# Delta-rule heads of a diffusion block on one Trainium2 core: directions dense on the partitions, paired 64x64 products, the next head's preparation inside the scan

## The reference, cut to what matters

```
qkv = silu(centred_conv(qkv, conv_w[l]))
q = l2norm(q) * DK ** -0.5;  k = l2norm(k)
o_f, s_f = gated_delta_chunked(q, k, v, beta[0], g[0], s0[:, 0])
o_b, s_b = gated_delta_chunked(rev(q), rev(k), rev(v), rev(beta[1]), rev(g[1]), s0[:, 1])
o = rmsnorm(o_f + rev(o_b), dn_norm[l]) * silu(z)
```

```
tmat = eye + bc[..., :, None] * einsum(kc, kc) * dec_strict
sol = triangular_solve(tmat, concat([(bc * gam) * kc, bc * vc]))
wk, uv = sol[..., :DK], sol[..., DK:]
u_c = uv_c - wk_c @ s
o_c = gam_c * (q_c @ s) + aqk_c @ u_c
s = gend_c * s + kd_c.T @ u_c
```

## Time and profile before

| | |
|---|---|
| runs | 4628.4, 4628.9, 4632.2 us; median 4628.9 |
| profiled execution | span 4630.4 us from the first to the last instruction, between the lowest and the highest run; what lies around the span cannot be told apart from that spread |
| instructions | 60884 |
| busy | PE 3719.1 us (80%), PEld 2456.7 (53%), DVE 2039.8 (44%), ACT 1080.3 (23%), POOL 890.1 (19%) |
| head phase | from 282.6 us to about 2196 us of the span, 1913 us |

### The profile page before, as it was taken

The page is one execution under the profiler, slowest core; times in us unless marked ns, Lnnn a source line. Parts: engine busy times, 40 slices in busy tenths (PEclk is TensorE's granted clock), DMA queues, the critical chain, the costliest instruction groups (busy, mean ns, idle before and its releaser), DMA issues. The chain is left out here.

```text
span 4630.4 us, 60884 instructions
## 1 busy us (share of the span) xinstructions
PE 3719.1 (80%) x22132; PEld 2456.7 (53%) x22398; DVE 2039.8 (44%) x3322; ACT 1080.3 (23%) x1702; POOL 890.1 (19%) x1040
## 2 busy tenths in 40 slices
PE   6568788888888797976854544599999699999997
PEld 2237575756666666755444444355454355555554
DVE  1236565656556565655459999422311211111112
ACT  0323232333232323232210011133211321111112
POOL 0010000000000000000067788011111011111110
PEclk8789898898989898989876777799999899999998
DMA  6210000000000000000311111221112011111111
GB/s 244 71 33 1 11 17 11 17 11 17 11 17 10 19 10 19 10 18 8 96 40 25 24 27 26 94 86 59 41 36 85 20 41 37 41 41 39 38 35 56
DMA packets 224662, 178.59 MB, mean 39 GB/s; under 512 B 24005, under 2 KB 211478, under 8 KB 222166
## 3 DMA queue, kind: packets, MB, share of 16 engines
q1 hardware_dynamic: 218214, 153.89, 11.4%
q10 hardware_dynamic: 4608, 11.54, 0.6%
q0 software_dynamic: 1648, 10.54, 0.6%
HBM read 144.39 MB, written 27.33 MB: 37 GB/s over the span
## 5 line engine op out<-in xcount | busy, mean ns | idle before, releaser
L171 POOL TENSOR_TENSOR w_pair<-w_raw,w_pair 128x1024 bf16<-128x1024 f32 (+1 forms) x156 | 345.9, 2220 | 2542.1 <-ACT w_pair L166 2542.1
L182 PE MATMUL m_out<-hn,w_pair 128*128 128x512 bf16 (+1 forms) x3102 | 569.3, 343 | 36.3 <-PEq L152 32.9
L182 PE MATMUL bank<-hn,w_pair 128*128 128x512 bf16 (+1 forms) x2220 | 480.3, 361 | 93.7 <-ACTq L1086 71.5
L182 PEld LDWEIGHTS m_out<-hn,w_pair 128*128 128x128 bf16 x3168 | 310.3, 98 | 294.9 <-issue 34.5
L182 PEld LDWEIGHTS bank<-hn,w_pair 128*128 128x128 bf16 x2304 | 225.8, 102 | 296.9 <-issue 131.3
L182 PE MATMUL m_out<-ys,w_pair 128*128 128x512 bf16 (+1 forms) x1552 | 288.6, 346 | 16.9 <-DVE ys L1996 15.0
L166 ACT ACTIVATE w_pair<-w_raw 128x1024 bf16<-128x1024 f32 x156 | 163.0, 1050 | 413.5 <-PE m_out L182 254.2
L1992 DVE TENSOR_TENSOR m_a<-m_out,m_sg 128x1280 f32<-128x1280 f32 x22 | 32.8, 1492 | 483.7 <-PE m_out L182 483.7
L1688 PE MATMUL s_banks<-u_block,m_block 128*128 128x160 f32 x128 | 40.9, 412 | 250.2 <-DVEq L1794 250.2
L182 PEld LDWEIGHTS m_out<-ys,w_pair 128*128 128x128 bf16 x1584 | 156.0, 99 | 149.6 <-issue 21.3
L182 PE MATMUL b_out<-ys,w_pair 128*128 128x512 bf16 (+1 forms) x1132 | 210.5, 345 | 5.2 <-PEq L1242 4.0
(11 more groups left out here) (346 smaller groups left out, 6460.6 us busy)
## 6 DMA issues: line engine op xcount, KB each, us to landing
w_raw<-in_w_in SPq DMA_DIRECT2D x56, 512.0 KB, 3.9
w_ada_rows<-in_w_ada SPq DMA_DIRECT2D x16, 1536.0 KB, 6.6
w_raw<-in_w_gu SPq DMA_DIRECT2D x44, 512.0 KB, 3.9
w_raw<-in_w_down SPq DMA_DIRECT2D x16, 512.0 KB, 4.0
scratch_x<-x_t POOLq DMA_DIRECT2D x1, 5120.0 KB, 16.4
scratch_o<-o_pair ACTq DMA_DIRECT2D x8, 640.0 KB, 3.9
scratch_u<-u_rows ACTq DMA_DIRECT2D x8, 640.0 KB, 2.9
u_block<-scratch_u SPq DMA_DIRECT2D x128, 40.0 KB, 1.8
```

The source lines that it names most:

```text
L171: pool.tensor_tensor(K.w_pair[:, slot, 1, 0:kt, :], K.w_raw[:, slot, 0:kt, :], K.w_pair[:, slot, 0, 0:kt, :], ALU.subtract).then_inc(K.w_l ...
L182: mm = pe.matmul(out[:, c0:c0 + cn], K.w_pair[:, slot, w, k, :], x[:, a, k, c0:c0 + cn], start=i < 3, stop=i >= 9 * kt - 3)
```

## The change

`phase_heads` is rewritten, and what it takes from `phase_decays` with it (beta times the decay to the chunk's end is made there, the order of packs follows the scan's order).

- Dense directions. The forward matrix of a pack lies on partitions 0 to 63, the backward one on 64 to 127, each 64 columns wide: x, xt, w and the masked matrices are 128 x 20 x 64, half as many columns. A product is issued as a pair, one matmul per direction, on the array's 64x64 tile of its half; the pair of the inverse, of uv and of at by u writes two partition halves of one bank, the pairs of wk and of kd by u write two banks.
- Groups. The inverse goes in four groups of five packs (320 columns). The mask of a level is applied by POOL to mt ahead of the level (`masked`); DVE adds the identity to the first product (`evict_v`) and copies xt; ACT copies x (`copy_x`). POOL scales k (`scale`).
- z. The z tile is put in ten parts between the products of levels 1 to 5 (`z_part`).
- Scan. One instruction for u over all partitions, one output add for two steps. The next head's decay differences, its k, q and v tiles (8 matmuls at each of 27 places from step 0 on), its squares, sums and norms are in it.
- Tail. Square, sums, gate and split of a head are done within levels 1 to 4 of the next one.
- No `head_end`; the loop over heads is written out in full. Every bank has its own semaphore; one ring of five banks. State is kept twice; POOL issues its loads, ACT its stores in the scan.

The core of the diff (PE, ACT and DVE of the scan, PE of the inverse):

```diff
-                        for g in range(NG):
-                            pe.wait_ge(s.inv, NG * (LEVELS * h + l - 1) + g + 1)
-                            for t in range(4):
-                                mm = pe.matmul(b[:, t, :], mt[:, 4 * g + t, :], xi[:, 4 * g + t, :], start=True, stop=True)
...
+                    for l in range(1, LEVELS):
+                        for g, t0, n in FIVES:
+                            pe.wait_ge(s.m, NF * (LEVELS * h + l) + g + 1)
+                            pe.wait_ge(s.x, NF * ((LEVELS - 1) * h + l - 1) + g + 1)
+                            b = to_write(pe, "v", h, l, g)
+                            for t in range(n):
+                                for d in range(2):
+                                    mm = pe.matmul(cols(b, C)[half(d), t, :], m_[half(d), l % 2, t0 + t, :], x[half(d), t0 + t, :], start=True, stop=True)
+                            mm.then_inc(full[b], 1)
+                        if l == 1:
+                            turn_v(h)
+                            if h:
+                                rms(h - 1)
+                        z_part(h, 2 * l - 2)
+                        for g, t0, n in FIVES:
...
+                            if l < LEVELS - 1:
...
+                                        mm = pe.matmul(cols(b, C)[half(d), t, :], xt[half(d), t0 + t, :], w_[half(d), t0 + t, :], start=True, stop=True)
...
+                                    mm = pe.matmul(cols(b, C)[half(d), t, :], w_[half(d), t0 + t, :], xt[half(d), t0 + t, :], start=True, stop=True)
...
+                        z_part(h, 2 * l - 1)
...
+                        bs = [to_write(pe, "kdu", h, i, d) for d in range(2)]
+                        pe.wait_ge(s.u, NSTEP * h + i + 1)
+                        for d in range(2):
+                            pe.matmul(bank[:, bs[d], 0:P], kd[half(d), i, :], u[half(d), i % 2, :], start=True, stop=True).then_inc(full[bs[d]], 1)
+                        for d in range(2):
+                            mm = pe.matmul(o[half(d), 2 * (i % 2) + 1, :], mtat[half(d), i, 1, :], u[half(d), i % 2, :], start=True, stop=True)
...
+                    if point == 0:
+                        pick_decays(h)
+                    for t, first_point in enumerate((1, 10, 19)):
+                        if first_point <= point < first_point + 9:
+                            tile_part(h, t, 8 * (point - first_point), 8)
+                    if point == 29:
+                        sums(h, 0)
+                    if point == 33:
+                        sums(h, 1)
...
+                    for p in range(NSTEP // 2):
+                        if n < H:
+                            if p == 4:
+                                copy_raw(n, 1)
+                            if p == 6:
+                                copy_raw(n, 2)
+                            if p == 8:
+                                inv_norm(n, 1)
+                        scale_q(h, p)
...
+                            if p == 6:
+                                high_part(n + 1, 0)
+                                inv_norm(n, 0)
+                                silu_square(n, 1)
...
+                        dve.tensor_tensor(u[:, i % 2, :], uv[:, i, :], bank[:, b, 0:P], ALU.subtract).then_inc(s.u, 1)
...
+                        if i % 2:
+                            b = to_read(dve, "o", h, i // 2)
+                            dve.wait_ge(s.oq, NSTEP * h + i + 1)
+                            dve.tensor_tensor(op[:, i - 1:i + 1, :], op[:, i - 1:i + 1, :], v[:, 1:4:2, :], ALU.add).then_inc(s.o, 1)
+                        elif i and not turned_by_act(i // 2 - 1):
+                            turned_o(h, i // 2 - 1)
+                        if n < H:
+                            if i == 0:
+                                decays(n)
+                            elif i >= 5:
+                                conv_tap(n, (i - 5) // 5, (i - 5) % 5)
+                            if i == 16:
+                                norm(n, 0)
...
+                    turned_o(h, NSTEP // 2 - 1)
+                    if n < H:
+                        norm(n, 1)
```

More of the change, by code:

```diff
@@ L763, in phase_heads, with to_write, to_read @@
+        def to_write(pe, *key):
+            if pl.before[key]:
+                pe.wait_ge(*emptied(*pl.before[key]))
+            return pl.at[key][0]
+        def to_read(eng, *key):
+            b, n = pl.at[key]
+            eng.wait_ge(full[b], n + 1)
+            return b
+        mt_needed = lambda t0, n: (t0 + n + 3) // 4
         with nc.Block() as block:
@@ new lines, in z_part, with rms, products @@
+                def z_part(h, point):
+                    tile_part(h, 3, 72 * point // 10, 72 * (point + 1) // 10 - 72 * point // 10)
+                def rms(h):
+                    pe.wait_ge(s.o_sq, h + 1)
+                    for m, (c0, cn) in enumerate(CHUNKS):
+                        b = to_write(pe, "rms", h, m)
+                        pe.matmul(bank[:, b, 0:cn], K.ones[:, :], sqo[:, c0:c0 + cn], start=True, stop=True).then_inc(full[b], 1)
+                def products(h):
+                    par = 1 + h % 2
+                    pe.wait_ge(s.normed, 2 * h + 2)
+                    for g, t0, n in GROUPS:
+                        b = to_write(pe, "kk", h, g)
+                        for t in range(n):
+                            for d in range(2):
+                                c = chunks_of(t0 + t)[d]
+                                mm = pe.matmul(cols(b, P)[half(d), t, :], kq[:, 0, c, :], kq[:, 0:par + 1:par, c, :], start=True, stop=True)
+                        mm.then_inc(full[b], 1)
@@ L969, in head @@
[L969 to L976 removed]
+                            pe.matmul(o[half(d), 2 * (i % 2), :], kq[:, 1 + par, chunks_of(i)[d], :], state[:, par, q, d, :], start=True, stop=True)
@@ L982, in _ @@
-                head(H - 1, False)
+                for j in range(2):
+                    sums(0, j)
+                for h in range(H):
+                    products(h)
+                    inverse(h)
+                    solve(h)
+                    scan(h)
+                rms(H - 1)
             @block.scalar
@@ new lines, in silu_v @@
+                def silu_v(h):
+                    act.wait_ge(s.tap, 15 * h + 15)
+                    if h:
+                        act.wait_ge(s.u, NSTEP * h)
+                    for d in range(2):
+                        for packs, prompt, chunks in segments(d):
+                            src = toks(a[0], T0, NC_P) if prompt else toks(a[0], 0, NC_S)
+                            i = act.activation(vt[:, packs, half(d)], src[:, chunks], ACT.Silu)
+                    i.then_inc(s.silu_v, 1)
@@ L1103, in _ @@
-                act.wait_ge(s.s_store, 32 * (H + 1))
+                decays(0)
+                copy_raw(0, 0)
+                high_part(0, 2)
+                copy_raw(0, 1)
+                high_part(0, 3)
+                silu_square(0, 0)
+                copy_raw(0, 2)
+                high_part(1, 0)
+                inv_norm(0, 0)
+                silu_square(0, 1)
+                inv_norm(0, 1)
+                for h in range(H):
+                    head(h)
+                rms_square(H - 1)
```

1073 lines of the change are left out of this document (580 added, 493 removed).

## The result

The changed kernel takes **4255.6 us** (median of 4 runs, 4254.3 to 4256.7), the kernel before in the same session 4628.6 (4620.2 to 4632.2): a ratio of 0.920, 95% interval 0.9188 to 0.9211. The forecast was 4235, in a range of 4065 to 4510. The profiled execution has a span of 4252.5 us.

What follows compares the result with a forecast made beforehand. PE bounds levels and mostly the scan; front and tail wait on ACT and DVE. First projections 75, eight heads 632, seven scans 742, last scan 67: 1516 against 1913, plus 2 for copies, giving 4235 us; range 4065 to 4510.

Steps and rivals of the forecast that it cites:

- The pair: Inverse's 64x64 matmul pair, one per direction: 0.13 us taken, between 0.11 below and 0.32 above.
- The first rival: The pair does not share the array: 0.224 us a pair, program 4517 us; chance 12%.
- The second rival: Small tiles cost more than full ones: 0.32 us a pair, program 4723, slower than before from 0.295; chance 6%.
- Products and level 1: Head's start: products with level 0 13 us, including 2.7 for the 0.50 clock; level 1 17.2 us.
- the 2 us for full banks in level 1: Level 1: PE's five banks stay full until ACT has done the rms logarithms and both table loads, 2 us.
- Solve: Stage after level 5: ACT sets it with table load, Silu, weight split, six copies and waits, 8.2 us.
- Scan, steps 0 to 13: Filled steps 4.4 us, step 0 7.0, two PE waits of about 0.8 for the tile copy: 65.8 us.
- The scan's end: After step 13 ACT's order rules: chain of adds waiting for scalings, 36.4 us, plus about 3.8 for lower clock.
- the lump of 3.8: Scan's end: about 3.8 us added to the chain's 36.4 for the lower clock.
- The rival of the shorter end: ACT's tables and logarithms run beside the scan's steps: scan near 90 us, program 4123; chance 20%.
- The rival of the lengthened scan: Next head's work not hidden: u waits behind the tap on DVE, filled step 5.4 us, program 4382; chance 17%.
- The last scan: Last head's scan without tiles: 2.2 us a step, 44 in all, then 23 for tail and last output.

Runs made afterwards that it cites:

- experiment 2: Changed kernel with only ACT's instruction order in the scan edited, scalings moved ahead of next-head work: 4174.4 us, ratio to before 0.9026.
- blocks of two: Changed kernel with the inverse's two directions issued in turn by blocks of two packs (2, 2, 1) instead of pack by pack: 4254.6 us.
- blocks of five: Changed kernel with the inverse's five products of one direction queued ahead of the five of the other, levels 1 to 5: 4366.8 us.

## Why the prediction came out as it did

The sign, the mechanism and the period hold: 185 forecast, 187.7 measured. Of the 17.5 us between forecast and span, seven periods make 16, the last head 8, the first projections -1, and the stretches outside the heads -6, which I did not follow. That the time came within half a per cent is partly luck: up to its scan a head is 3.4 us shorter than forecast, its scan 6.2 longer.

- **The pair.** 0.13 taken, 0.117 measured: on 60 pairs the 0.8 us by which levels 2 to 4 are shorter (10.0 to 10.2 for 10.8). No row of before showed such a pair, so 0.13 was a choice between 0.11 and 0.32 and not a reading. The first rival is refuted. By the rule of the Trainium skill, TensorEngine Tiling (Array Packing), section Restrictions and Gotchas, that different row tiles cannot access one PSUM bank at the same time, it would have been right; the records 0.006 us apart differ from that rule, and the measurement decides for pairs that write different partitions of the bank. The second rival, 0.295 and more, falls with it.
- **Products and level 1.** 13 and 17.2 forecast, 13.4 and 14.9 measured. A POOL mask takes 0.935 us for 0.79 (L874, 192 in the page's groups), eight of them 1.2; the 2 us for full banks in level 1 didn't come. The terms listed on the path of the products add up to 9.7, not 10.3, so the forecast had 0.6 more than they give.
- **Solve.** 8.2 forecast with ACT as its bound, 9.2 measured with PE as its bound: PE is busy 9.20 of 9.20. The step that failed named ACT's six copies and gave PE no price: 40 pairs at the forecast's own 0.22 are 8.8, more than its 8.2. 20 pairs of uv and 20 of wk take 4.5 and 4.7, 0.23 a pair, and ACT waits for them. wk costs as much as uv although only 64 columns move through it: its passes start 0.111 us apart, and not 0.058 as in the inverse: as far apart as the loads of its 128 weight columns.

```profile
1171.22 4.58 PE L1049 MATMUL bank<-vt,xx 64*64 64x128 f32 x80
...
1175.74 4.68 PE L1056 MATMUL bank<-xx,gk 64*128 64x64 f32 x80
1175.86 0.60 ACT L1254 ACTIVATE vt<-bank 128x512 f32<-128x512 f32 x1 [0.28 <-PE bank L1049]
```

  Up to the scan 75.6 for 79, where the terms too high and too low partly cancel.
- **Scan, steps 0 to 13.** 65.8 forecast, 70.5 measured to the start of step 14. A filled step without turns was 4.22 by the terms and takes 4.40 in steps 7 and 13, since eight projection matmuls with the return to the small tiles of the array take 1.51 and not 1.42. The turns fall on every second step and cost some 0.3 there, as their 0.16 a step had it: steps of 4.7 to 4.8, and 5.1 in step 12, where u is late. PE's two waits for the tile copy make steps of 5.3 and 5.5. Step 0 took 8.6 for 7.0: PE waits 2.04 us for DVE's subtraction and then runs its first eight projection matmuls in 2.7 us instead of 1.4; the granted clock of that step is 0.85. In head 4 of the run with z in one piece it stayed at 1.00, and step 0 took 7.26.

```profile
1180.40:1189.00 8.60, 6.49 (x31) 3.08 (x30) 2.72 (x5) 1.70 (x3) 2.88 (x1) 0.85 0.00 0
...
1186.33 2.74 PE L182 MATMUL bank<-hn,w_pair 128*128 128x512 bf16 x7 [2.04 <-DVE dt L1331]
```

- **The scan's end.** 40.2 forecast, 41.7 measured. The chain was told rightly: DVE's output adds of steps 13, 15 and 17 wait 3.19, 5.58 and 1.84 us for ACT, and experiment 2 removes most of that, which takes 10 us a head away. The pieces are less exact: the sums of k and of q took 4.4 and 3.5 us at a low clock for 2.2, which the lump of 3.8 was to cover, and from the u of step 17 to the next products it is 16.0 for 13.6. The rival of the shorter end (scan 90) did not come; with the better order the scan is still 100 to 102. The rival of the lengthened scan asked for filled steps of 5.4 on DVE; they take 4.4 to 4.8, 5.1 in step 12, and more only where PE waits for the tile copy.
- **The last scan.** 44 forecast for twenty steps, 56.2 measured for nineteen and 58.6 for all: the term that was most wrong. I took a step of the last scan before and left out one instruction; the clock in that row was 1.00, and I gave the new, thinner step the same. It was granted 0.50 from 1749.5 us on, in step 2. At 1.00 nineteen steps take 44.1 and twenty 45.7, near the forecast. The row was also one of the shorter steps: the whole of that scan took 56.1 us, 2.8 a step and not 2.53.

```profile
2121.40:2177.50 56.10, 37.58 (x300) 28.53 (x300) 30.04 (x100) 10.39 (x30) 0.00 (x0) 1.00 0.00 1
```


## What to carry to other kernels

Two small fp32 products on opposite corners of the array cost what one does, if they stand within about two products of each other in PE's queue; issue them in turn. When work of a next stage is moved beside a serial scan, the price is paid by whatever engine serves both in order: put the instruction that the scan needs ahead of the moved one (71 us here over seven heads, for an edit of ACT's order alone). And forecast a thin PE stretch at both clock levels, since the row it is taken from may have had the other.

## What was not expected of the hardware

The sharing of the array reaches across a few queue entries: three passes of a block of ten ran beside the block ahead (seven passes from start to start), and blocks of four lost nothing.

The clock of one and the same instruction stream differed from kernel to kernel, between its two levels, 1.00 (2.4 GHz) and 0.50 (1.2 GHz). In the profiled executions the last scan was granted 1.00 throughout in the three kernels with ACT's order changed and no added matmuls. The clock fell to 0.50 in step 6 with z in level 1, in step 5 with blocks of two, and in step 2 in the changed kernel and in those with blocks of five and with the tail put back. Only what ran earlier, and with it the moment at which the scan began, was different; which of the two decides was not separated. So a forecast from the rows of before could not tell on which side such a stretch would fall. A few full-width matmuls in the gaps, 160 in all, held it at 1.00 in both runs that had them. The Trainium skill, TensorE: Matmul & The Clock Gate, section Part 1: The HAM clock gate, says that the gate's observation runs free and does not start anew with the kernel. The different steps in which the clock fell fit that, but do not show it.
